# The last four V blocks by token block, the gathered block between the steps, and LayerNorm's scale and shift in two VectorE passes

## The chip, the cores and the metric

One core of a Trainium2 chip runs the whole kernel. The metric is the device time of one execution in microseconds, as the median of several runs. A profile belongs to one execution, whose own time is given beside its span.

## What is computed

The kernel is one layer of an encoder over 512 tokens of width 1024: LayerNorm, a mixer (gated linear recurrence and short convolution), LayerNorm, a PEER expert layer with 16384 one-neuron experts, LayerNorm. The change lies in the end of the expert layer and in the last LayerNorm:

```python
def layer_norm(x, g, b):
    xf = x.astype(jnp.float32)
    mu = jnp.mean(xf, axis=-1, keepdims=True)
    var = jnp.mean(jnp.square(xf - mu), axis=-1, keepdims=True)
    y = (xf - mu) * lax.rsqrt(var + LN_EPS) * g.astype(jnp.float32) + b.astype(jnp.float32)
    return y.astype(x.dtype)

def expert_block(args):
    xb, ib, gb = args
    u = u_tab[ib].astype(x.dtype)
    act = jax.nn.gelu(jnp.einsum("cd,ced->ce", xb, u), approximate=False)
    v = v_tab[ib].astype(x.dtype)
    return jnp.einsum("ce,ced->cd", gb * act, v)

f = peer(h, peer_wq[l], peer_k1[l], peer_k2[l], peer_u[l], peer_v[l])
h = layer_norm(ALPHA * h + f, ln2_g[l], ln2_b[l])
```

## The kernel before

The 512 tokens are four token blocks of 128. For the first three (DT = 3, DTOK = 384 tokens) the expert layer is computed densely: the 16384 experts are 128 blocks of 128 rows, and for each block the activations (gelu of x times the U rows) are multiplied by a matrix of gates and then by the V rows. The fourth block, called gathered here (index DT, `far` in the code), fetches its own rows: GpSimd issues one indirect DMA for each of its 128 slots in either table (L790, L795), and VectorE multiplies and adds them (L808 for U, L812 for V, into the two tiles `gather_sum`).

Stages are blocks of code in which each engine has its own instruction list (L229, L861, L1063, L1334); engines meet at the end of each, where every queue drains. The change lies in the last stage, `experts` (L1241). Its 128 steps take one V block each. Up to TAIL = 64 every second step also makes the activations of a block; from 64 on the steps only load them. The last gathered tile is used in step 111 (TAIL + tail_tiles = 112). Order within a step n is written out by hand for each engine:

- SyncE (L1354): loads of v_raw and g_in for step n + 4 (SLOT = 4 buffers), and of a_in for the step after the next.
- ScalarE (L1432): v_hi of step n + 2 (L1430, float32r half of the V block, waits for y_done of step n - 2, since the four buffers go round), then w_hi of step n (L1449).
- VectorE (L1501): a gathered tile, w = activation times gate (L1520), v_lo of step n + 2 (L1498), w_lo of step n (L1525).
- TensorE (L1407): outputs(n - 1) (L1390): for each of three token blocks and each of the products w_hi v_hi, w_hi v_lo, w_lo v_hi, two matmuls of 512 columns (L1400), 18 in all, accumulated in two PSUM banks per token block. It waits for v_lo and w_lo of its step. In the last step y_ready is raised after each token block.

Then comes the end. VectorE first works on the gathered block (L1535, L1537: 2^0.25 h plus the two sums; L1549, L1551: mean and variance), then on each dense block when y_ready has come (L1545, L1549, L1551). For each block GpSimd computes 1/sqrt(var + eps) and the shift in four operations on one column (L1485 to L1488), ScalarE applies them to 1024 columns (L1458), and the learned scale and shift are two passes (L1327, L1328) that are split by columns: 768 on VectorE (LEFT), 256 on GpSimd (RIGHT). SyncE stores each part (L1383). `Chain` (L76) makes an engine wait for the end of its own instruction. `LAST` is the order of the blocks: gathered, 0, 1, 2.

Of the kernel before, what the change touches and what calls it, by code (L numbers as in the profile page):

```python
# [31 lines left out]
P = 128  # L32
# [1208 lines left out]
def experts(nc, a, sem, bank, h, small, acts, far, act_dram, gates_dram, out):  # L1241
# [9 lines left out]
    STEPS = KEYS  # L1251
    GATHERS = 2 * TURN
# [4 lines left out]
    assert u_turns * GATHERS == SLOTS - U_FROM and 0 <= tail_tiles <= STEPS - TAIL  # L1257
    LAST = (DT, *range(DT))
    LEFT, RIGHT = slice(0, 6 * P), slice(6 * P, D)
# [10 lines left out]
    with ExitStack() as st:  # L1270
# [13 lines left out]
        shift = sb("shift2", [P, TB, 1])  # L1284
# [7 lines left out]
        ln2_loaded, var_ready, rstd_ready, norm_ready, stored = (sem(n) for n in (  # L1292
            "ln2_loaded", "var2_ready", "rstd2_ready", "norm2_ready", "out_stored"))
        y_ready, left_ready, right_ready = sem("y_block_ready"), sem("out_left_ready"), sem("out_right_ready")
        chain, pool_chain = sem("dve_chain_experts"), sem("pool_chain_experts")
# [38 lines left out]
        with nc.Block() as block:  # L1334
            @block.sync
            def _(eng):
# [50 lines left out]
            def _(eng):  # L1387
                mm = nc.tensor.matmul

                def outputs(n, i):  # L1390

                    first, last = (isinstance(n, int) and n == e for e in (0, STEPS - 1))
                    r = i % SLOT
                    eng.wait_ge(v_lo_ready, n + 1)
                    eng.wait_ge(w_lo_ready, n + 1)
                    for tb in range(DT):
                        for w, v, begins, ends in ((w_hi, v_hi, first, False), (w_hi, v_lo, False, False),
                                                   (w_lo, v_hi, False, last)):
                            for half in range(2):
                                ins = mm(bank[2 + 2 * tb + half][:, :], w[r][:, tb * P:(tb + 1) * P],  # L1400
                                         v[r][:, half * HALF_D:(half + 1) * HALF_D], start=begins, stop=ends)
                        if last:
                            ins.then_inc(y_ready, 1)
                    if not last:
                        ins.then_inc(y_done, 1)

                def step(n, i, t, tiles):  # L1407
# [8 lines left out]
                    if not (isinstance(n, int) and n == 0):  # L1416
                        outputs(n - 1, i - 1)

                steps(eng, step)
                outputs(STEPS - 1, STEPS - 1)  # L1420

            @block.scalar
            def _(eng):
# [8 lines left out]
                def step(n, i, t, tiles):  # L1432
# [23 lines left out]
                for at, tb in enumerate(LAST):  # L1456
                    eng.wait_ge(rstd_ready, at + 1)
                    S.activation(h[:, tb, :], h[:, tb, :], ACT.Identity, scale=rs[:, tb, :],  # L1458
                                 bias=shift[:, tb, :]).then_inc(norm_ready, 1)

            @block.gpsimd
            def _(eng):
# [16 lines left out]
                link = Chain(eng, pool_chain)  # L1479
                eng.wait_ge(ln2_loaded, 32)  # L1480
                for at in range(TB + 1):
                    if at < TB:
                        tb = LAST[at]
                        eng.wait_ge(var_ready, at + 1)
                        link(G.tensor_tensor(out=rs[:, tb, :], in0=mv[:, tb, 1:2], in1=small[:, 2:3], op=ALU.add))  # L1485
                        link(G.tensor_tensor(out=rs[:, tb, :], in0=rs[:, tb, :], in1=small[:, 0:1], op=ALU.pow))  # L1486
                        link(G.tensor_tensor(out=shift[:, tb, :], in0=mv[:, tb, 0:1], in1=rs[:, tb, :], op=ALU.mult))
                        G.tensor_tensor(out=shift[:, tb, :], in0=shift[:, tb, :], in1=small[:, 1:2],  # L1488
                                        op=ALU.mult).then_inc(rstd_ready, 1)
                    if at:  # L1490
                        affine(eng, G, link, at - 1, RIGHT, right_ready)

            @block.vector
            def _(eng):
# [6 lines left out]
                def step(n, i, t, tiles):  # L1501
# [20 lines left out]
                    if not (isinstance(n, int) and n + 2 >= STEPS):  # L1522
                        v_lower(n + 2, i + 2)
                    eng.wait_ge(w_hi_ready, n + 1)
                    V.tensor_tensor(out=w_lo[i % SLOT][:, :], in0=w32[:, i % 2, :], in1=w_hi[i % SLOT][:, :].bitcast(F32),  # L1525
                                    op=ALU.subtract).then_inc(w_lo_ready, 1)
                    if more:
                        acts.lower_half(eng, 1, m + 1, r + 1, 0)

# [3 lines left out]
                link = Chain(eng, chain)  # L1533
                eng.wait_ge(ln2_loaded, 32)
                link(V.scalar_tensor_tensor(out=h[:, DT, :], in0=h[:, DT, :], scalar=ALPHA, in1=far.sum[0][:, :],  # L1535
                                            op0=ALU.mult, op1=ALU.add))
                link(V.tensor_tensor(out=h[:, DT, :], in0=h[:, DT, :], in1=far.sum[1][:, :], op=ALU.add))  # L1537
                for at in range(TB + 1):
                    if at < TB:
                        tb = LAST[at]  # L1540
                        if at:
                            eng.wait_ge(y_ready, at)
                            for i in range(2):
                                blk = h[:, tb, i * HALF_D:(i + 1) * HALF_D]
                                ins = V.scalar_tensor_tensor(out=blk, in0=blk, scalar=ALPHA, in1=bank[2 + 2 * tb + i][:, :],  # L1545
                                                             op0=ALU.mult, op1=ALU.add)
                            link(ins)
                        for i in range(2):
                            ins = V.bn_stats(bn[:, tb, i, :], h[:, tb, i * HALF_D:(i + 1) * HALF_D])  # L1549
                        link(ins)  # L1550
                        V.bn_aggr(mv[:, tb, :], bn[:, tb, :, :].rearrange("p a b -> p (a b)")).then_inc(var_ready, 1)  # L1551
                    if at:
                        affine(eng, V, link, at - 1, LEFT, left_ready)
# [23 lines left out]
```

## Time and profile before

| | us |
|---|---|
| median of 3 runs | 1810.9 (1807.27 to 1812.17) |
| profiled execution | 1810.05 |
| its span | 1808.2 |
| TensorE busy in the span | 1690.4 (93%) |
| VectorE busy | 1337.9 (74%) |
| GpSimd busy | 977.7 (54%) |
| ScalarE busy | 740.4 (41%) |

Engines are PE (TensorE matmul), PEld (its weight loads, beside PE), DVE (VectorE), ACT (ScalarE), POOL (GpSimd) and SP (SyncE); a q behind a name is the engine's queue. L12 is line 12 of the kernel. In brackets stands how long the engine sat idle before an instruction, and what released it. Starts and ends are in microseconds from the start of the span; PEclk is the granted TensorE clock as a share of full speed, 2.4 GHz.

### The profile page before, as it was taken

To read this page: it belongs to the slowest core of one execution; us is meant where nothing else is said; L and a number is where in the kernel's file an instruction comes from. 1 tells how busy PE (TensorE), PEld (TensorE's weight loads), DVE (VectorE), ACT (ScalarE), POOL (GpSimd) and SP (SyncE) were. 2 spreads that over 40 slices of the span, in tenths; PEclk is the share of its full clock that TensorE was granted. 3 is DMA by queue.
4 is the path that set the end of the run, shared out by engine and by line. 5 is a ranking of instruction groups with operands and counts; after the bars stand their busy time and mean duration, and the time that the engine had idled before them with its cause. 6 is when DMAs were issued, how large, how long until landed. Compare 5 with 4: busy or idle time off the path is not lost. (4 is left out here: it accounts for less than half of the span.)

```text
span 1808.2 us, 27242 instructions
## 1 busy us (share of the span) xinstructions
PE 1690.4 (93%) x8781; PEld 1461.1 (81%) x8781; DVE 1337.9 (74%) x2430; ACT 740.4 (41%) x1188; POOL 977.7 (54%) x844
## 2 busy tenths in 40 slices
PE   5998889799998999999989997999999999999995
PEld 4776644499998999888988896888888888888884
DVE  7469952368889998599589806778778777888756
ACT  2458750323335455444544443333333333333332
POOL 5635430184436666677667753444666666555303
PEclk8999999899999999999999998999999999999998
DMA  8322100333324557877977798998999989999971
GB/s 263 123 76 70 53 0 0 131 111 111 105 72 136 170 175 252 268 231 226 307 228 232 225 347 316 319 329 311 319 324 322 318 292 328 362 351 356 325 228 62
DMA packets 224428, 396.76 MB, mean 219 GB/s; under 512 B 15256, under 2 KB 155472, under 8 KB 224336
## 3 DMA queue, kind: packets, MB, share of 16 engines
q1 hardware_dynamic: 182512, 258.12, 41.9%
q0 software_dynamic: 36864, 134.23, 22.6%
q10 hardware_dynamic: 4960, 3.24, 0.6%
q8 instruction: 50, 0.82, 0.2%
q14 instruction: 42, 0.34, 0.1%
HBM read 349.40 MB, written 46.14 MB: 219 GB/s over the span
## 5 line engine op out<-in xcount | busy, mean ns | idle before, releaser
L748 POOL TENSOR_TENSOR ut_lo<-gather_sum,ut_hi 128x512 fp32r<-128x512 f32 x194 | 263.3, 1377 | 199.3 <-ACT gather_sum L728 197.9
L708 PE MATMUL bank<-xhi,ut_hi 128*128 128x384 f32 x1024 | 355.8, 347 | 0.0
L708 PE MATMUL bank<-xhi,ut_lo 128*128 128x384 f32 x1024 | 345.1, 337 | 0.0
L708 PE MATMUL bank<-xlo,ut_hi 128*128 128x384 f32 x1024 | 344.7, 337 | 0.0
L1498 DVE TENSOR_TENSOR v_lo<-v_raw,v_hi 128x1024 fp32r<-128x1024 f32 x128 | 156.2, 1220 | 120.8 <-ACT v_hi L1430 120.8
L1400 PE MATMUL bank<-v_hi,w_hi 128*128 128x512 f32 x768 | 241.0, 395 | 4.4 <-DVE w_lo L1525 4.4
L795 POOL DMA_INDIRECT gathered<-in_peer_v,row_index x128 | 182.1, 1423 | 106.5 <-POOLq L794 101.9
L790 POOL COPY row_index<-expert_rows 128x1 int32 (+1 forms) x256 | 174.4, 681 | 120.8 <-DVE gather_product L808 60.0
L1400 PE MATMUL bank<-v_lo,w_hi 128*128 128x512 f32 x768 | 238.0, 391 | 0.0
L1400 PE MATMUL bank<-v_hi,w_lo 128*128 128x512 f32 x768 | 237.2, 390 | 0.0
L1430 ACT ACTIVATE v_hi<-v_raw 128x1024 fp32r<-128x1024 f32 x128 | 135.6, 1059 | 245.9 <-PE bank L1400 234.8
L795 POOL DMA_INDIRECT gathered<-in_peer_u,row_index x128 | 151.3, 1182 | 104.1 <-POOLq L794 103.0
L708 PEld LDWEIGHTS bank<-xlo,ut_hi 128*128 128x128 f32 x1024 | 194.2, 190 | 0.0
L708 PEld LDWEIGHTS bank<-xhi,ut_hi 128*128 128x128 f32 x1024 | 194.2, 190 | 0.0
L708 PEld LDWEIGHTS bank<-xhi,ut_lo 128*128 128x128 f32 x1024 | 193.4, 189 | 0.0
L808 DVE SCALAR_TENSOR_TENSOR gather_product<-gathered,h 128x1024 f32<-128x1024 f32 x128 | 172.9, 1351 | 16.5 <-DMA gathered<-in_peer_u,row_index 9.8
L725 ACT ACTIVATE ut_hi<-bank 128x512 fp32r<-128x512 f32 x256 | 154.9, 605 | 73.1 <-PE bank L696 72.9
L1124 DVE TENSOR_SCALAR first<-iota,selT 128x128 f32<-128x128 f32 x384 | 183.8, 545 | 0.0
L1400 PEld LDWEIGHTS bank<-v_lo,w_hi 128*128 128x128 f32 x768 | 144.8, 188 | 30.8
L1400 PEld LDWEIGHTS bank<-v_hi,w_lo 128*128 128x128 f32 x768 | 144.5, 188 | 30.7
L1400 PEld LDWEIGHTS bank<-v_hi,w_hi 128*128 128x128 f32 x768 | 142.3, 189 | 32.6 <-DVE v_lo L1498 5.0
L696 PE MATMUL bank<-ident,u_raw 128*128 128x128 f32 x1024 | 142.8, 276 | 25.9 <-POOL ut_lo L748 15.7
(182 smaller groups left out, 2855.0 us busy)
## 6 DMA issues: line engine op xcount, KB each, us to landing
u_raw<-in_peer_u SPq DMA_DIRECT2D x128, 512.0 KB, 5.3
v_raw<-in_peer_v SPq DMA_DIRECT2D x128, 512.0 KB, 5.7
g_in<-gate_matrix SPq DMA_DIRECT2D x128, 192.0 KB, 4.2
activations<-gel SPq DMA_DIRECT2D x96, 192.0 KB, 2.0
a_in<-activations SPq DMA_DIRECT2D x96, 192.0 KB, 4.5
gate_matrix<-stage SPq DMA_DIRECT2D x15, 1152.0 KB, 8.0
w_in<-in_w_in SPq DMA_DIRECT2D x28, 512.0 KB, 3.8
wq<-in_peer_wq SPq DMA_DIRECT2D x16, 512.0 KB, 4.2
```

The source lines that it names most:

```text
L696: ins = self.nc.tensor.transpose(self.bank[b][:, k * P:(k + 1) * P], raw[:, j * P:(j + 1) * P], self.ident[:, :])
L708: ins = self.nc.tensor.matmul(self.bank[b + (r % 2) * spare][:, 0:DTOK], u[r % 2][:, k, :], x[:, k, 0:DTOK], start=(i == 0), stop=(i == 3 ...
L725: ins = self.nc.scalar.activation(self.hi[r % 2][at], turned, ACT.Copy)
L748: self.nc.gpsimd.tensor_tensor(out=self.lo[r % 2][at], in0=self.whole[at], in1=self.hi[r % 2][at].bitcast(F32), op=ALU.subtract).then_inc( ...
L790: nc.gpsimd.tensor_copy(self.index[r][:, :], self.rows[:, bass.ds(k, 1)]).then_inc(self.index_ready, 1)
L795: nc.gpsimd.indirect_dma_start(out=self.tile[r][:, :], out_offset=None, in_=self.tables[kind], in_offset=bass.IndirectOffsetOnAxis(ap=self ...
L808: ins = V.scalar_tensor_tensor(out=self.product[:, :], in0=self.tile[r][:, :], scalar=1.0, in1=self.x, op0=ALU.mult, op1=ALU.mult, accum_o ...
L1124: ins = V.tensor_scalar(out=first[:, u, q, :], in0=iota[:, :], scalar1=selT[:, 0, bass.ds(t + q, 1)], scalar2=selT[:, 2, bass.ds(t + q, 1) ...
L1400: ins = mm(bank[2 + 2 * tb + half][:, :], w[r][:, tb * P:(tb + 1) * P], v[r][:, half * HALF_D:(half + 1) * HALF_D], start=begins, stop=ends)
L1430: S.activation(v_hi[r][:, :], v_raw[r][:, :], ACT.Copy).then_inc(v_hi_ready, 1)
L1498: V.tensor_tensor(out=v_lo[r][:, :], in0=v_raw[r][:, :], in1=v_hi[r][:, :].bitcast(F32), op=ALU.subtract).then_inc(v_lo_ready, 1)
```

## The change

- TensorE: the last four steps (CLOSE = 124 on) are no longer done one V block after the other. `closing` takes token block 0 for all four V blocks, then token block 1, then 2, and raises y_ready after each. The waits for v_lo and w_lo of the four steps all stand in token block 0.
- ScalarE and VectorE: v_hi and v_lo of step 127 move from step 125 to step 126, behind w_hi and w_lo of that step.
- The gathered block's residual, statistics, centring and scaling (`far_block`) go into steps 113 to 117 of VectorE, one part at the end of each step.
- The last LayerNorm is (h - mean) * gain and then * rstd + bias, each one scalar_tensor_tensor on VectorE, the second in two halves of 512 columns. VectorE adds epsilon. GpSimd keeps only the power of -0.5, ScalarE has no part.
- SyncE stores halves of 512 columns.

```diff
+    CLOSE = STEPS - SLOT
+    FAR_DONE = TAIL + tail_tiles
-        def affine(eng, engine, link, at, cols, ready):
-            blk = h[:, LAST[at], cols]
-            eng.wait_ge(norm_ready, at + 1)
-            link(engine.tensor_tensor(out=blk, in0=blk, in1=ln[:, 0, cols], op=ALU.mult))
-            engine.tensor_tensor(out=blk, in0=blk, in1=ln[:, 1, cols], op=ALU.add).then_inc(ready, 1)
@@ SyncE @@
                 for at, tb in enumerate(LAST):
-                    for cols, ready in ((RIGHT, right_ready), (LEFT, left_ready)):
-                        eng.wait_ge(ready, at + 1)
+                    for half in range(2):
+                        cols = slice(half * HALF_D, (half + 1) * HALF_D)
+                        eng.wait_ge(out_ready, 2 * at + half + 1)
                         eng.dma_start(out[0, tb * P:(tb + 1) * P, cols], h[:, tb, cols]).then_inc(stored, 16)
@@ TensorE @@
+                def closing():
+                    for tb in range(DT):
+                        for n in range(CLOSE, STEPS):
+                            if tb == 0:
+                                eng.wait_ge(v_lo_ready, n + 1)
+                                eng.wait_ge(w_lo_ready, n + 1)
+                            ins = block_outputs(tb, n % SLOT, False, n == STEPS - 1)
+                        ins.then_inc(y_ready, 1)
-                    if not (isinstance(n, int) and n == 0):
+                    if not (isinstance(n, int) and (n == 0 or n > CLOSE)):
                         outputs(n - 1, i - 1)
                 steps(eng, step)
-                outputs(STEPS - 1, STEPS - 1)
+                closing()
@@ ScalarE @@
-                    if not (isinstance(n, int) and n + 2 >= STEPS):
+                    if not (isinstance(n, int) and n + 2 >= STEPS - 1):
                         v_upper(n + 2, i + 2, loads)
                     S.activation(w_hi[i % SLOT][:, :], w32[:, i % 2, :], ACT.Copy).then_inc(w_hi_ready, 1)
+                    if isinstance(n, int) and n == STEPS - 2:
+                        v_upper(n + 1, i + 1, (n + 1) // SLOT + 1)
-                for at, tb in enumerate(LAST):
-                    eng.wait_ge(rstd_ready, at + 1)
-                    S.activation(h[:, tb, :], h[:, tb, :], ACT.Identity, scale=rs[:, tb, :],
-                                 bias=shift[:, tb, :]).then_inc(norm_ready, 1)
@@ GpSimd @@
-                for at in range(TB + 1):
...
+                for at, tb in enumerate(LAST):
+                    eng.wait_ge(var_ready, at + 1)
+                    G.tensor_tensor(out=rs[:, tb, :], in0=rs[:, tb, :], in1=small[:, 0:1],
+                                    op=ALU.pow).then_inc(rstd_ready, 1)
@@ VectorE, in a step @@
-                    if not (isinstance(n, int) and n + 2 >= STEPS):
+                    if not (isinstance(n, int) and n + 2 >= STEPS - 1):
                         v_lower(n + 2, i + 2)
...
+                    if isinstance(n, int) and n == STEPS - 2:
+                        v_lower(n + 1, i + 1)
+                    if isinstance(n, int) and FAR_DONE <= n < FAR_DONE + 6:
+                        far_block(n - FAR_DONE)
@@ VectorE, the parts @@
+                def moments(tb):
+                    for i in range(2):
+                        ins = V.bn_stats(bn[:, tb, i, :], h[:, tb, i * HALF_D:(i + 1) * HALF_D])
+                    link(ins)
+                    link(V.bn_aggr(mv[:, tb, :], bn[:, tb, :, :].rearrange("p a b -> p (a b)")))
+                    V.tensor_scalar(out=rs[:, tb, :], in0=mv[:, tb, 1:2], scalar1=LN_EPS, scalar2=None,
+                                    op0=ALU.add).then_inc(var_ready, 1)
+                def centre(tb):
+                    link(V.scalar_tensor_tensor(out=h[:, tb, :], in0=h[:, tb, :], scalar=mv[:, tb, 0:1], in1=ln[:, 0, :],
+                                                op0=ALU.subtract, op1=ALU.mult))
+                def spread(tb):
+                    eng.wait_ge(rstd_ready, LAST.index(tb) + 1)
+                    for half in range(2):
+                        cols = slice(half * HALF_D, (half + 1) * HALF_D)
+                        V.scalar_tensor_tensor(out=h[:, tb, cols], in0=h[:, tb, cols], scalar=rs[:, tb, :],
+                                               in1=ln[:, 1, cols], op0=ALU.mult, op1=ALU.add).then_inc(out_ready, 1)
+                def far_block(part):
+                    if part == 1:
+                        link(V.scalar_tensor_tensor(out=h[:, DT, :], in0=h[:, DT, :], scalar=ALPHA, in1=far.sum[0][:, :],
+                                                    op0=ALU.mult, op1=ALU.add))
+                    elif part == 2:
+                        link(V.tensor_tensor(out=h[:, DT, :], in0=h[:, DT, :], in1=far.sum[1][:, :], op=ALU.add))
+                    elif part == 3:
+                        moments(DT)
+                    elif part == 4:
+                        eng.wait_ge(ln2_loaded, 32)
+                        centre(DT)
+                    elif part == 5:
+                        spread(DT)
+                for tb in range(DT):
+                    eng.wait_ge(y_ready, tb + 1)
...
+                    moments(tb)
+                    centre(tb)
+                    spread(tb)
```

## Rows read from the trace of the kernel before

**Rows 1.** The page's head.

```profile
span 1808.2 us, 27242 instructions
```

**Rows 2.** Chain that ended last, in order of time: start us, us, what.

```profile
1525.02 0.14 issue
1525.16 258.67 PE bank L1400 x1140
...
1801.52 1.35 POOLq L1334
```

**Rows 3.** Instructions of L1334: duration ns min/median/max, first and last start us.

```profile
L1334 POOLq DRAIN  x1: 6499/6499/6499, 1801.5 to 1801.5; - x1
...
L1334 SPq DRAIN  x1: 7/7/7, 1805.9 to 1805.9; - x1
```

**Rows 4.** The same of L1063, the stage before.

```profile
L1063 POOLq DRAIN  x1: 8546/8546/8546, 1081.9 to 1081.9; - x1
```

**Rows 5.** Timeline of GpSimd at the end of L1063's stage: start us, us.

```profile
1080.95 2.54 POOL L748 TENSOR_TENSOR ut_lo<-gather_sum,ut_hi 128x512 fp32r<-128x512 f32 x2 [2.53 <-ACT gather_sum L728]
```

**Rows 6.** Timeline of all engines, 1783 to 1799 us: start us, us, what.

```profile
1783.85 1.28 DVE L1545 SCALAR_TENSOR_TENSOR h<-h,bank 128x512 f32<-128x512 f32 x2 [3.56 <-PE bank L1400]
...
1793.00 1.28 DVE L1545 SCALAR_TENSOR_TENSOR h<-h,bank 128x512 f32<-128x512 f32 x2
...
1794.31 1.29 DVE L1549 BATCH_NORM_STATS2 bn<-h 128x6 f32<-128x512 f32 x2
...
1795.63 0.21 DVE L1551 BATCH_NORM_AGGREGATE mv<-bn 128x2 f32<-128x12 f32 x1
...
1796.70 0.96 DVE L1328 TENSOR_TENSOR h<-h,ln 128x768 f32<-128x768 f32 x1
1796.79 1.27 POOL L1486 TENSOR_TENSOR rs<-rs,small 128x1 f32<-128x1 f32 x1
```

**Rows 7.** Timeline of TensorE, 1770 to 1775 us, two of its rows: block starts.

```profile
1770.05 0.62 PE L1400 MATMUL bank<-v_hi,w_hi 128*128 128x512 f32 x2
...
1774.13 0.62 PE L1400 MATMUL bank<-v_hi,w_hi 128*128 128x512 f32 x2
```

**Rows 8.** Timeline of VectorE and ScalarE, 1768 to 1776 us.

```profile
1768.93 0.55 DVE L1520 TENSOR_TENSOR w<-a_in,g_in 128x384 f32<-128x384 f32 x1
...
1770.31 1.06 ACT L1430 ACTIVATE v_hi<-v_raw 128x1024 fp32r<-128x1024 f32 x1 [2.61 <-PE bank L1400]
...
1771.40 1.23 DVE L1498 TENSOR_TENSOR v_lo<-v_raw,v_hi 128x1024 fp32r<-128x1024 f32 x1 [1.92 <-ACT v_hi L1430]
...
1772.54 0.55 DVE L1525 TENSOR_TENSOR w_lo<-w,w_hi 128x384 fp32r<-128x384 f32 x1
...
1773.01 0.55 DVE L1520 TENSOR_TENSOR w<-a_in,g_in 128x384 f32<-128x384 f32 x1
...
1773.59 0.53 ACT L1449 ACTIVATE w_hi<-w 128x384 fp32r<-128x384 f32 x1 [1.81 <-DVE w L1520]
...
1774.15 0.56 DVE L1525 TENSOR_TENSOR w_lo<-w,w_hi 128x384 fp32r<-128x384 f32 x1 [0.59 <-ACT w_hi L1449]
```

**Rows 9.** DMA issues, 1768 to 1776 us: xcount, KB each, median us to landing.

```profile
a_in<-activations SPq DMA_DIRECT2D x1, 192.0 KB, 3.4
```

**Rows 10.** Timeline, 1516 to 1519 us: VectorE's L812 beside GpSimd's L790.

```profile
1516.71 1.28 DVE L812 SCALAR_TENSOR_TENSOR gather_sum<-gathered,expert_gates,gather_sum 128x1024 f32<-128x1024 f32 x1 [0.28 <-DMA gathered<-in_peer_v,row_index]
...
1517.28 0.75 POOL L790 COPY row_index<-expert_rows 128x1 int32<-128x1 int32 x1
```

**Rows 11.** Instructions of L535: duration ns min/median/max.

```profile
L535 DVE TENSOR_SCALAR rms<-bank x2: 151/157/163, 267.2 to 267.2; 128x4 f32<-128x4 f32 x2
```

**Rows 12.** Stretches: length, busy us (x) PE PEld DVE ACT POOL, PEclk, DMA, GB/s.

```profile
952.00:957.10 5.10, 2.99 (x25) 2.80 (x25) 4.96 (x12) 1.14 (x3) 3.57 (x4) 1.00 0.60 202
1039.00:1042.80 3.80, 0.89 (x6) 0.68 (x7) 0.00 (x0) 1.16 (x3) 3.46 (x3) 0.99 1.11 348
1042.80:1046.20 3.40, 3.40 (x14) 3.40 (x13) 0.00 (x0) 1.51 (x3) 2.56 (x2) 0.51 1.05 389
```

More of the change, by code:

```diff
@@ L1291, in experts @@
         y_done = sem("y_step_done")
[L1292 to L1295, printed above, removed]
+        ln2_loaded, var_ready, rstd_ready, stored = (sem(n) for n in (
+            "ln2_loaded", "var2_ready", "rstd2_ready", "out_stored"))
+        y_ready, out_ready = sem("y_block_ready"), sem("out_half_ready")
+        chain = sem("dve_chain_experts")
         def steps(eng, step, between=lambda: None):
@@ L1390, in outputs @@
                 def outputs(n, i):
-                    first, last = (isinstance(n, int) and n == e for e in (0, STEPS - 1))
-                    r = i % SLOT
+                    first = isinstance(n, int) and n == 0
                     eng.wait_ge(v_lo_ready, n + 1)
@@ L1396, in outputs, with block_outputs @@
                     for tb in range(DT):
[L1397 to L1405, printed above, removed]
+                        ins = block_outputs(tb, i % SLOT, first, False)
+                    ins.then_inc(y_done, 1)
+                def block_outputs(tb, r, first, last):
+                    for w, v, begins, ends in ((w_hi, v_hi, first, False), (w_hi, v_lo, False, False),
+                                               (w_lo, v_hi, False, last)):
+                        for half in range(2):
+                            ins = mm(bank[2 + 2 * tb + half][:, :], w[r][:, tb * P:(tb + 1) * P],
+                                     v[r][:, half * HALF_D:(half + 1) * HALF_D], start=begins, stop=ends)
+                    return ins
+                def closing():
[6 more added lines that the diff above has]
+                        ins.then_inc(y_ready, 1)
                 def step(n, i, t, tiles):
@@ L1526, in step @@
                                     op=ALU.subtract).then_inc(w_lo_ready, 1)
+                    if isinstance(n, int) and n == STEPS - 2:
+                        v_lower(n + 1, i + 1)
                     if more:
                         acts.lower_half(eng, 1, m + 1, r + 1, 0)
+                    if isinstance(n, int) and FAR_DONE <= n < FAR_DONE + 6:
+                        far_block(n - FAR_DONE)
+                link = Chain(eng, chain)
+                def moments(tb):
[10 more added lines that the diff above has]
+                    eng.wait_ge(rstd_ready, LAST.index(tb) + 1)
+                    for half in range(2):
+                        cols = slice(half * HALF_D, (half + 1) * HALF_D)
[14 more added lines that the diff above has]
+                        spread(DT)
                 v_lower(0, 0)
@@ L1532, in _ @@
                 steps(eng, step, between=lambda: far.weigh(eng))
[L1533 to L1553, printed above, removed]
+                for tb in range(DT):
+                    eng.wait_ge(y_ready, tb + 1)
+                    for i in range(2):
+                        blk = h[:, tb, i * HALF_D:(i + 1) * HALF_D]
+                        ins = V.scalar_tensor_tensor(out=blk, in0=blk, scalar=ALPHA, in1=bank[2 + 2 * tb + i][:, :],
+                                                     op0=ALU.mult, op1=ALU.add)
+                    link(ins)
+                    moments(tb)
+                    centre(tb)
+                    spread(tb)
 _INS = ["x", "ln_emb_g", "ln_emb_b", "w_in", "lru_conv_w", "lru_conv_b", "lru_wa", "lru_ba", "lru_wx", "lru_bx",
```

16 lines of the change are left out of this document (1 added, 15 removed).

## Prediction

> **What bounds the kernel now.** I read the end of the chain of waits first. Its last long piece is TensorE's matmuls of L1400; after those it runs over VectorE and GpSimd, and its last piece is GpSimd's queue at 1801.52 us [rows 1, 2]. So up to the last matmul TensorE sets the time, and behind it the LayerNorm of the last blocks. Next I read the instructions of L1334, where each engine closes the stage. GpSimd's last arithmetic ends at 1801.52 + 1.35 = 1802.87 us, but its closing DRAIN runs to 1808.05 us (start 1801.5, 6.499 long), 0.15 before the end of the span; SyncE is through at 1805.9 [rows 1 to 3]. The closing of GpSimd, 5.18 us after its last arithmetic, is what ends last. The stage before has the same picture: last GpSimd instruction over at 1083.49 us, DRAIN over at 1081.9 + 8.55 = 1090.45, so 6.96 us later [rows 4, 5]. The time is therefore matmuls, then a serial stretch from the first finished token block (VectorE starts on it at 1783.85) to GpSimd's last instruction, 19.02 us, then 5.33 us of closing [rows 1, 2, 6].
>
> In that stretch VectorE has three token blocks one after the other, and then the last one's way over GpSimd and ScalarE is left.
>
> **Token blocks first.** A V block takes 18 matmuls, 4.08 us from the start of one block to the next, 0.2267 us a matmul [rows 7]. Today token block 0 is complete after 60 of the last 72 matmuls, afterwards after 24. That is 36 x 0.2267 = 8.16 us earlier: 1783.85 - 8.16 = 1775.69 us. Blocks 1 and 2 follow 24 matmuls, 5.44 us, apart: 1781.13 and 1786.57. The number of matmuls and of weight loads stays, so this moves no TensorE time.
>
> **What it demands.** The closing part wants V blocks 124 to 127 within 5.44 us: from its start at 1770.05 us, block 125 at 1771.41, 126 at 1772.77, 127 at 1774.13 [rows 7]. Here the order on ScalarE and VectorE counts. Until w of step 125 (1768.93) nothing changes. Then w_hi(125) no longer stands behind v_hi(127) (1770.31). The steps between starts are, from the rows: w to w_hi 0.58, w_hi to w_lo 0.56, w_lo to the next w 0.47, v_hi to v_lo 1.09, v_lo to the next VectorE instruction 1.14 [rows 8]. So w_hi(125) 1769.51, w_lo(125) 1770.07, w(126) 1770.55, w_hi(126) 1771.13, w_lo(126) 1771.69, over at 1772.25: in time for 125 and 126. On ScalarE v_hi(127) now stands behind w_hi(126) and starts at about 1771.63; behind it are queued v_lo(127) 1772.72, w(127) 1773.86, w_hi(127) 1774.44, w_lo(127) 1775.00. That ends at 1775.55, and with the 0.14 us that the chain shows from the end of a w_lo to the matmul it releases, just ahead of its long piece [rows 2], TensorE can go on at 1775.69 instead of 1774.13. I count a wait of 1.56 us. It shifts the three readiness times to 1777.25, 1782.69 and 1788.13. SyncE's last activation load takes 3.4 us to land [rows 9]; it is released by w(125), over at 1769.48, whose time does not change, so it is there at about 1772.9, ahead of 1773.86.
>
> **The gathered block between steps.** It comes out of the stretch behind the matmuls, where its last two passes lie between the dense blocks, and goes into steps 113 to 117 of VectorE. There VectorE stands idle for 1.92 us in each step before v_lo [rows 8]. The parts are 1.22 to 1.28 us for one pass over 1024 columns [rows 10], and about 1.71 us for the statistics (1.32 + 0.23 + 0.16, below). Each fits into the 1.92; behind them queue w of the next step and, if a part ran over, v_lo and w_lo. w_lo(125) ends 1.04 us before its matmuls at 1774.13, so there are 0.9 us of spare on top [rows 7, 8]. Cost nothing; if the cover were gone, all parts together are 1.24 + 1.24 + 1.71 + 1.30 + 1.34 = 6.8 us. Its two output transfers move ahead of the others on SyncE, at about 1774.4, when the loads are over, and hold nothing up. GpSimd's single pow for it waits with nothing queued behind but the later pows.
>
> **The LayerNorm of blocks 0 to 2.** Per block on VectorE, start to start [rows 6]: residual add 1.31, statistics 1.32, the aggregate with a wait for its end 0.21 + 0.02 = 0.23. Then the new addition of epsilon on a 128x1 tile. The nearest row is a TENSOR_SCALAR of 128x4, 0.157 us [rows 11]; consecutive instructions overlap by 0.09 (v_lo ends 1772.63, w_lo starts 1772.54), so 0.07; bounds 0.05 and 0.23, the aggregate's. Centring, one pass with a scalar from a tile: 1.28 as L812 [rows 10], over two operands in SBUF like that one. Then the wait for GpSimd's pow. The same pow stood beside a multiplication of VectorE from two SBUF tiles: L1328 ends at 1797.66, the pow at 1798.06, so it did its work, 0.40 us, only after VectorE had finished [rows 6]. L790's copy beside L812 shows the same: started 1517.28, over at 1518.03, right behind L812's end 1517.99 [rows 10]. So 0.40, and I take 0.06 to hand over. Last the two halves with the second scalar, 1.34, 1.25 to the next block's start. Sum 1.31 + 1.32 + 0.23 + 0.07 + 1.28 + 0.46 + 1.25 = 5.92 us.
>
> The Trainium skill, SBUF — State Buffer, section "Who interferes with whom", says that a VectorE instruction with two SBUF inputs and a GpSimd instruction that reads SBUF exclude each other for the whole instruction, whoever comes first. The pow rows agree with it. By that rule the 0.46 us is paid in each block, since the centring is issued before the pow can be; without it the pow would be hidden, and that case is the second rival below.
>
> **The sum.** Block 0 starts at 1777.25; block 1 at 1783.17 (its matmuls are over at 1782.69); block 2 at 1789.09 (1788.13). VectorE is what limits here, by 0.5 to 1 us. GpSimd's last pow ends 1.31 + 1.32 + 0.23 + 0.07 + 1.28 + 0.40 = 4.61 us later, at 1793.70, instead of 1802.87: 9.17 us less. Of this 6.60 is the earlier start (8.16 - 1.56), and 2.57 the shorter stretch (16.45 for 19.02). SyncE: last half written at 1795.1; from the last piece ready (1802.87) to its end (1805.9) it took 3.03 us, so 1798.1. GpSimd's DRAIN, 5.18 us after its last work, ends 1798.9 and still sets the end. The profiled execution took 1810.05 us, 1.85 more than its span; less 9.17 this gives 1800.9 us. The median of the three runs is 1810.9, their mean 1810.1, so I do not shift it.
>
> **Rivals.**
> 1. The DRAIN is longer or hangs on the last transfer. With the 6.96 us of the stage before [rows 4, 5] the time is 1802.7; counted from SyncE's end (1808.05 - 1805.9 = 2.15) it is 1798.1 + 2.15 + 0.15 = 1800.4 of span, 1802.3. For it: two DRAINs of different length and no row that says what they wait for.
> 2. The pow slips in under the centring. A block is 5.46 us, the starts 1782.71 and 1788.17, GpSimd over by 1792.4 at the latest: 1799.5. Against it: the pow rows.
> 3. TensorE's wait lets the granted clock fall. From 952.0 to 957.1 us TensorE was busy for 2.99 of 5.10 us and the clock stayed at 1.00, that is 2.4 GHz; from 1039.0 it was busy for 0.89 of 3.80 us, and then the clock was 0.51, 1.2 GHz, for the 3.4 us from 1042.8 [rows 12]. The forecast's wait of 1.56 us between full stretches is nearer to the first. If it fell, 3.4 us at half speed cost 1.7 us, of which 0.5 hide behind VectorE: 1802.1.
> 4. The closing does not follow GpSimd's last work at all, and the end stays at 1810, or the gathered block's cover fails and eats 6.8 us: 1807.7. Against the first: the DRAIN here is open until 2.15 us behind SyncE, with nothing else left to wait for [rows 3].
> 5. Slower. The one mechanism: the last activation tile lands so late that TensorE stands in the closing part and then does the 54 matmuls left at half clock, 54 x 0.2267 = 12.2 us more. Block 2 would be ready at 1800.4, GpSimd over at 1805.0: 1812.2 even with the wait of 1.56. It counts as slower once the wait passes 4.9 us, a landing of about 7.7 us instead of 3.4, in the middle 1816. Against it: the 3.4, and 0.9 us to spare.
>
> **How the numbers follow.** Forecast 0.60; rival 1 0.12; rival 2 0.08; rival 3 0.07; rival 4 0.10; rival 5 0.03. About 0.3% is what a measurement here can tell, 5.4 us, so faster means under 1805.5. The first four cases are faster, 0.87; rival 4 is within, 0.10; slower 0.03. The range takes rivals 1 to 3, with their sizes added on the high side (1800.9 + 1.8 + 1.2 = 1803.9) and 1799.5 on the low; the three runs lie 3.6 below to 1.3 above their median, so I widen by 1 to 2 us: 1797.5 to 1805.0.
>
> **What would show it.** Right: a wait of about 1.5 us on TensorE before block 127's first matmul, released by w_lo; VectorE's first residual add at about 1777.3, blocks 5.9 us apart; GpSimd's pows ending 0.4 us behind the centring; VectorE idle in steps 113 to 117 shrunk from 1.92 us without a gap on TensorE; the DRAIN ending 5.2 us behind the last pow. Wrong: a DRAIN that ends 7 us behind, or at a fixed distance from the transfers; a granted clock of 0.5 before the last matmul; a gap on TensorE before step 124.

## Result: 1799.05 us, and the profile after

| | before | changed |
|---|---|---|
| median of 8 runs, us | 1810.14 (1805.89 to 1814.72) | 1799.05 (1798.07 to 1801.95) |
| profiled execution, us | 1810.05 | 1799.0 |
| its span, us | 1808.2 | 1797.2 |
| first matmul of V block 124, us from the start of the span | 1770.05 | 1767.79 |
| from there to the end of the span, us | 38.2 | 29.4 |

The ratio of the changed kernel to the one before is 0.9945, with a 95% interval of 0.9932 to 0.9958, so 10.0 us less, with 2.4 to either side. The forecast was 1800.9.

The two last lines of the table cut the profile in two. The change touches nothing ahead of step 113, and what lies ahead of V block 124 differs by 2.26 us all the same. The rest, 8.8 us, lies behind it. I call that part the stretch below; it is what the forecast had summed to 9.17.

The timeline of all engines of the changed kernel, from the closing part on. Columns: start us, us, engine, line, operation, tiles, and in brackets the idle time before and what ended it.

```profile
1767.79 0.62 PE L1398 MATMUL bank<-v_hi,w_hi 128*128 128x512 f32 x2
...
1769.30 1.04 ACT L1435 ACTIVATE v_hi<-v_raw 128x1024 fp32r<-128x1024 f32 x1
...
1772.66 0.56 DVE L1519 TENSOR_TENSOR w_lo<-w,w_hi 128x384 fp32r<-128x384 f32 x1 [0.59 <-ACT w_hi L1454]
1773.37 0.70 PE L1398 MATMUL bank<-v_hi,w_hi 128*128 128x512 f32 x2 [1.34 <-DVE w_lo L1519]
...
1775.03 1.29 DVE L1574 SCALAR_TENSOR_TENSOR h<-h,bank 128x512 f32<-128x512 f32 x2 [1.81 <-PE bank L1398]
...
1776.35 1.29 DVE L1533 BATCH_NORM_STATS2 bn<-h 128x6 f32<-128x512 f32 x2
...
1777.67 0.21 DVE L1535 BATCH_NORM_AGGREGATE mv<-bn 128x2 f32<-128x12 f32 x1
1777.92 0.16 DVE L1536 TENSOR_SCALAR rs<-mv 128x1 f32<-128x1 f32 x1
1777.99 1.28 DVE L1541 SCALAR_TENSOR_TENSOR h<-h,mv,ln 128x1024 f32<-128x1024 f32 x1
...
1778.15 1.53 POOL L1484 TENSOR_TENSOR rs<-rs,small 128x1 f32<-128x1 f32 x1 [45.57 <-DVE rs L1536]
...
1779.79 1.42 DVE L1549 SCALAR_TENSOR_TENSOR h<-h,rs,ln 128x512 f32<-128x512 f32 x2 [0.53 <-POOL rs L1484]
...
1781.13 1.28 DVE L1574 SCALAR_TENSOR_TENSOR h<-h,bank 128x512 f32<-128x512 f32 x2
...
1787.20 1.28 DVE L1574 SCALAR_TENSOR_TENSOR h<-h,bank 128x512 f32<-128x512 f32 x2
...
1790.31 1.52 POOL L1484 TENSOR_TENSOR rs<-rs,small 128x1 f32<-128x1 f32 x1 [4.55 <-DVE rs L1536]
1791.94 1.41 DVE L1549 SCALAR_TENSOR_TENSOR h<-h,rs,ln 128x512 f32<-128x512 f32 x2 [0.52 <-POOL rs L1484]
```

Read it downwards. v_hi(127) starts right behind w_hi(126), without the wait that it had before [rows 8]; w_lo(127) ends at 1773.22. TensorE had finished its share of block 126 by then and stood idle for 1.34 us; it goes on 0.15 us later with block 127. VectorE starts on token block 0 at 1775.03, 7.24 us into the stretch; before it was 13.8 [rows 6, 7]. From then on its rows follow each other, but for 0.53 us behind each centring, in which it waits for GpSimd's pow.

The closing instructions of the last stage, same kernel (duration in ns, minimum, median and maximum, then first and last start in us); they answer to [rows 3]:

```profile
L1327 POOLq DRAIN  x1: 6702/6702/6702, 1790.3 to 1790.3; - x1
...
L1327 SPq DRAIN  x1: 7/7/7, 1795.6 to 1795.6; - x1
```

GpSimd's DRAIN ends at 1797.0, 5.14 us behind the end of its last pow (1791.83), and 1.3 us behind SyncE. It still ends last.

The gathered block between the steps, from the timeline of VectorE in steps 115 and 116 (the first three rows are the statistics of the gathered block, the other two belong to the step):

```profile
1729.95 1.28 DVE L1533 BATCH_NORM_STATS2 bn<-h 128x6 f32<-128x512 f32 x2
1731.26 0.21 DVE L1535 BATCH_NORM_AGGREGATE mv<-bn 128x2 f32<-128x12 f32 x1
1731.51 0.15 DVE L1536 TENSOR_SCALAR rs<-mv 128x1 f32<-128x1 f32 x1
1731.59 0.56 DVE L1514 TENSOR_TENSOR w<-a_in,g_in 128x384 f32<-128x384 f32 x1
1732.42 1.23 DVE L1492 TENSOR_TENSOR v_lo<-v_raw,v_hi 128x1024 fp32r<-128x1024 f32 x1 [0.28 <-ACT v_hi L1435]
```

Of the 1.92 us of idle time before v_lo 0.28 are left in the fullest step; v_lo still waits for ScalarE and not for the new work. From 1700 us to the end the only wait that the trace shows for TensorE is the one of 1.3 us before block 127, so the parts cost nothing.

### The profile page after: what moved, and what is told of

Its sections match the earlier page's. It is cut to its first block and busy times, and to the rows that moved or that the text cites. A ratio compares the mean times of both kernels' runs of the same rounds, so it can differ in the third digit from the quotient of the medians.

```text
span 1797.2 us, 27229 instructions
## 1 busy us (share of the span) xinstructions
PE 1691.6 (94%) x8781; PEld 1460.1 (81%) x8781; DVE 1343.7 (75%) x2438; ACT 735.0 (41%) x1184; POOL 971.6 (54%) x824
## 5 line engine op out<-in xcount | busy, mean ns | idle before, releaser
L790 POOL COPY row_index<-expert_rows 128x1 int32 (+1 forms) x256 | 181.4, 708 | 113.0 <-DVE gather_product L808 60.0
```

The lines of the kernel that those rows point to most:

```text
L790: nc.gpsimd.tensor_copy(self.index[r][:, :], self.rows[:, bass.ds(k, 1)]).then_inc(self.index_ready, 1)
```

## Experiments

Each kernel's profile is measured in the same way: the stretch runs from the first matmul of V block 124 to the end of the span. The edits are against the changed kernel unless it says otherwise. The last column is the median of the kernel before, run beside it.

| kernel | stretch, us | expected | median, us | before beside it, us |
|---|---|---|---|---|
| before | 38.2 | | | |
| changed | 29.4 | 29.0 by the forecast | 1799.05 | 1810.14 |
| e1, steps to the end | 36.0 | 36.0 | 1806.61 | 1809.36 |
| e2, block order alone | 34.0 | 33.9 | 1804.62 | 1809.36 |
| e3, v(127) in its old step | 30.3 | 30.2 | 1801.59 | 1809.36 |
| e6, gathered block at the end | 34.8 | 34.7 | 1806.9 | 1809.36 |
| e4, root on ScalarE | 27.2 | 27.1 | 1796.84 | 1808.62 |
| e5, late GpSimd instruction | 31.1 | 31.2 | 1802.38 | 1808.62 |
| e7, pow before centring | 29.0 | 29.9 to 30.3 | 1800.36 | 1808.62 |
| e8, e4 and split waits | 26.6 | 26.5 | 1798.42 | 1808.62 |
| e9, no gathers | 28.1 | 28.0 | 1783.94 (one run) | 1810.06 |
| e10, changed again | 29.4 | 29.4 | 1799.56 | 1810.06 |
| e11, e8 again | 26.6 | 26.6 | 1799.12 | 1810.06 |

### Which part brought it: e1, e2, e6

e1 takes back the order of the matmuls:

```diff
-                    for tb in range(DT):
-                        for n in range(CLOSE, STEPS):
-                            if tb == 0:
-                                eng.wait_ge(v_lo_ready, n + 1)
-                                eng.wait_ge(w_lo_ready, n + 1)
+                    for n in range(CLOSE, STEPS):
+                        eng.wait_ge(v_lo_ready, n + 1)
+                        eng.wait_ge(w_lo_ready, n + 1)
+                        for tb in range(DT):
...
-                        ins.then_inc(y_ready, 1)
+                            if n == STEPS - 1:
+                                ins.then_inc(y_ready, 1)
```

> The changed kernel with one part undone: V blocks 124 to 127 are multiplied one after the other again, y_ready still comes after each token block of the last. I measure from the first matmul of V block 124 to the end of the span: 38.15 us before, 29.41 us in the changed kernel. Theory (the order pays by starting VectorE earlier): TensorE has no wait before block 127, token block 0 is ready 13.8 us in instead of 7.24, VectorE's three blocks still take 6.08 us each, so the stretch is about 36.0 us, 6.5 us longer than the changed kernel and 2.2 shorter than before. Rival (VectorE's passes are the bound whatever the order, and the two-pass LayerNorm brought the gain): the stretch is 29.4 to 30.5 us.

The first matmul of block 124 and VectorE's first instruction on token block 0, from two answers of its timeline:

```profile
1771.65 0.39 PE L1398 MATMUL bank<-v_hi,w_hi 128*128 128x512 f32 x1
```

```profile
1785.45 0.69 DVE L1574 SCALAR_TENSOR_TENSOR h<-h,bank 128x512 f32<-128x512 f32 x1 [8.37 <-PE bank L1398]
```

VectorE starts 13.80 us in and had been idle for 8.37. The stretch is 36.0 us: without the order of the matmuls the two other parts together (gathered block and LayerNorm) are worth 2.2 us, and the order is worth 6.5 on top of them. The rival is out.

e2 is the kernel before with the order of the matmuls and the two moves of step 127 alone (`closing` is that of the change):

```diff
+    CLOSE = STEPS - SLOT
...
-                    if not (isinstance(n, int) and n == 0):
+                    if not (isinstance(n, int) and (n == 0 or n > CLOSE)):
                         outputs(n - 1, i - 1)
...
-                outputs(STEPS - 1, STEPS - 1)
+                closing()
...
+                    if isinstance(n, int) and n == STEPS - 2:
+                        v_upper(n + 1, i + 1, (n + 1) // SLOT + 1)
...
+                    if isinstance(n, int) and n == STEPS - 2:
+                        v_lower(n + 1, i + 1)
```

> The kernel before with one part of the change alone: the last four V blocks by token block, with v_hi and v_lo of step 127 behind w_hi and w_lo of step 126. The gathered block and the LayerNorm stay as before. Theory: VectorE reaches token block 0 only after the gathered block's parts, 9.5 us after the first matmul of block 124 and not at 7.24, so part of the 6.6 us is lost: stretch 33.9 us, 4.2 shorter than before. Rival (the parts add up): 6.6 us shorter than before, 31.5 us.

```profile
1768.82 1.22 DVE L1551 SCALAR_TENSOR_TENSOR h<-h,gather_sum 128x1024 f32<-128x1024 f32 x1
1769.04 0.70 PE L1405 MATMUL bank<-v_hi,w_hi 128*128 128x512 f32 x2 [1.34 <-DVE w_lo L1539]
```

These rows of its timeline show the collision. The matmuls of block 127 and the gathered block's first pass start at the same time; VectorE comes to token block 0 at 1772.78, 9.3 us after the first matmul at 1763.46, and not at 7.24. The stretch is 34.0 us, 4.2 less than before. The order alone thus keeps 4.2 of the 6.6 us it makes room for.

e6 puts the gathered block's parts behind the last step:

```diff
-                    if isinstance(n, int) and FAR_DONE <= n < FAR_DONE + 6:
-                        far_block(n - FAR_DONE)
...
                 steps(eng, step, between=lambda: far.weigh(eng))
+                for part in range(6):
+                    far_block(part)
```

> The changed kernel with the gathered block's five parts behind the last step of VectorE instead of in steps 113 to 117. Theory: they fill the 1.8 us in which VectorE waits for token block 0 and push it by the rest: 7.1 us of parts from the end of w_lo(127), token block 0 starts about 5.3 us later, the stretch is 34.7 us. Rival (the parts lie beside matmuls and cost nothing there either, as TensorE still has 11 us to go): stretch 29.4 to 30.5 us.

From VectorE's timeline:

```profile
1777.20 1.22 DVE L1553 SCALAR_TENSOR_TENSOR h<-h,gather_sum 128x1024 f32<-128x1024 f32 x1
...
1784.49 1.27 DVE L1574 SCALAR_TENSOR_TENSOR h<-h,bank 128x512 f32<-128x512 f32 x2
```

7.3 us of parts stand between the last step and token block 0, which starts 12.64 us into the stretch; the stretch is 34.8. That these parts lie beside busy matmuls is no help: VectorE is the engine that is late there. Moving them is worth 5.4 us once the order and the LayerNorm have changed. e6 also answers a question about the LayerNorm: with the gathered block at the end in both, the new LayerNorm has a stretch of 34.8 us and the old one 34.0 (e2), so there the new one, with the order of the gathered block's passes that goes with it, is 0.8 us slower.

### The wait that the order costs: e3, e8

e3 puts v_hi(127) and v_lo(127) back:

```diff
-                    if not (isinstance(n, int) and n + 2 >= STEPS - 1):
+                    if not (isinstance(n, int) and n + 2 >= STEPS):
...
-                    if isinstance(n, int) and n == STEPS - 2:
-                        v_upper(n + 1, i + 1, (n + 1) // SLOT + 1)
```

and the same for `v_lower`.

> The changed kernel with v_hi and v_lo of step 127 back in step 125. Theory: w_hi(125) and w_lo(125) stand behind v_hi(127) and v_lo(127) again, TensorE waits about 1.8 us before block 125 and a little before 126 and 127, 2.3 us together instead of 1.5; VectorE starts on token block 0 about 0.8 us later and the stretch is 30.2 us instead of 29.4. Rival (block 127's data set the wait in either order): no difference, 29.4 us with one wait of 1.5 us before block 127.

```profile
1772.70 0.70 PE L1398 MATMUL bank<-v_hi,w_hi 128*128 128x512 f32 x2 [1.67 <-DVE w_lo L1517]
...
1774.32 0.71 PE L1398 MATMUL bank<-v_hi,w_hi 128*128 128x512 f32 x2
...
1775.94 0.70 PE L1398 MATMUL bank<-v_hi,w_hi 128*128 128x512 f32 x2
```

In TensorE's timeline the first row is block 125, the others 126 and 127: three blocks come late, 1.62 us apart where 1.36 would do. VectorE starts 8.09 us in, the stretch is 30.3. The two moves are worth 0.8 us.

### GpSimd's pow and its DRAIN: e4, e5, e7, e9

e4 takes GpSimd out of the LayerNorm:

```diff
 @@ ScalarE @@
+                def root(tb):
+                    eng.wait_ge(var_ready, LAST.index(tb) + 1)
+                    S.activation(rs[:, tb, :], rs[:, tb, :], ACT.Sqrt).then_inc(rstd_ready, 1)
...
 @@ GpSimd @@
-                for at, tb in enumerate(LAST):
-                    eng.wait_ge(var_ready, at + 1)
-                    G.tensor_tensor(out=rs[:, tb, :], in0=rs[:, tb, :], in1=small[:, 0:1],
-                                    op=ALU.pow).then_inc(rstd_ready, 1)
 @@ VectorE, spread @@
                     eng.wait_ge(rstd_ready, LAST.index(tb) + 1)
+                    link(V.reciprocal(rs[:, tb, :], rs[:, tb, :]))
```

> The changed kernel without GpSimd in the LayerNorm: ScalarE takes the square root of variance plus epsilon, VectorE its reciprocal on one column, behind the centring. GpSimd's last work is then the last gather, long before. Two things are tested. Theory: the wait of 0.53 us behind each centring goes and a reciprocal of about 0.2 us comes, so the last half is written about 0.9 us earlier; and GpSimd's closing DRAIN, which follows GpSimd's last work by about 5.2 us, is out of the way, so that SyncE's end sets the time: the stretch from the first matmul of block 124 to the end is about 27.1 us instead of 29.41. Rival (the DRAIN ends at a fixed distance behind the output transfers or behind the other engines): it still ends 1.4 us or more behind SyncE, and the stretch is 28.5 us. Second rival (the wait behind the centring is the length of the pow, and the root on ScalarE takes as long): 29.0 us or more.

Its timeline, token block 0 from the centring on, and the closing instructions:

```profile
1777.63 1.28 DVE L1545 SCALAR_TENSOR_TENSOR h<-h,mv,ln 128x1024 f32<-128x1024 f32 x1
1777.75 0.20 ACT L1464 ACTIVATE rs<-rs 128x1 f32<-128x1 f32 x1 [5.47 <-DVE rs L1540]
1778.94 0.16 DVE L1551 RECIPROCAL rs<-rs 128x1 f32<-128x1 f32 x1
1779.14 1.41 DVE L1554 SCALAR_TENSOR_TENSOR h<-h,rs,ln 128x512 f32<-128x512 f32 x2
...
1780.47 1.28 DVE L1579 SCALAR_TENSOR_TENSOR h<-h,bank 128x512 f32<-128x512 f32 x2
```

```profile
L1327 POOLq DRAIN  x1: 9296/9296/9296, 1695.4 to 1695.4; - x1
...
L1327 SPq DRAIN  x1: 7/7/7, 1794.4 to 1794.4; - x1
```

The root runs wholly beside the centring, a block takes 5.80 us where it took 6.10, and the DRAIN was over at 1704.7, long before. SyncE sets the end, 0.2 us before the end of the span (1794.6). Both rivals are out.

e5 adds one instruction and nothing else:

```diff
+                eng.wait_ge(out_ready, 2 * TB)
+                G.memset(pool_tile[:, :], 0.0)
```

> The changed kernel with one memset of one column on GpSimd after the last output half is ready, a tile that nobody reads. Theory (the DRAIN ends about 5.2 us behind GpSimd's last instruction): that instruction ends about 1.7 us later than the last pow did, and the stretch grows from 29.4 to about 31.2 us. Rival (the DRAIN's end hangs on the transfers or on a fixed schedule): no difference, 29.4 us.

```profile
1793.88 0.10 POOL L1488 MEMSET pool_tile<- 128x1 f32 x1 [1.59 <-DVE h L1552]
```

```profile
L1328 POOLq DRAIN  x1: 5246/5246/5246, 1793.9 to 1793.9; - x1
...
L1328 SPq DRAIN  x1: 7/7/7, 1796.1 to 1796.1; - x1
```

A memset of 0.10 us makes the stretch 1.7 us longer. The DRAIN ends at 1799.1, again 5.1 us behind GpSimd's last instruction, while SyncE ends 27.8 us into the stretch as in the changed kernel. So it is GpSimd's last instruction that the end hangs on, and not the output transfers.

e7 makes VectorE wait for the pow ahead of the centring:

```diff
                 def centre(tb):
 
+                    eng.wait_ge(rstd_ready, LAST.index(tb) + 1)
                     link(V.scalar_tensor_tensor(out=h[:, tb, :], in0=h[:, tb, :], scalar=mv[:, tb, 0:1], in1=ln[:, 0, :],
```

> The changed kernel, but VectorE waits for GpSimd's pow before it starts the centring, so that nothing of VectorE runs beside the pow. Theory (the pow's 1.53 us are 0.57 us of work and the time in which VectorE's two SBUF inputs keep it out): each pow takes 0.57 us; VectorE waits about 0.8 us for it before the centring and not after, a block takes about 6.35 us instead of 6.08, the stretch 29.9 to 30.3 us. Rival (this pow takes 1.5 us whoever runs beside it): VectorE waits 1.7 us, a block takes 7.2 us, and the stretch is 32.5 us or more.

```profile
1780.05 0.56 POOL L1484 TENSOR_TENSOR rs<-rs,small 128x1 f32<-128x1 f32 x1 [45.57 <-DVE rs L1536]
1780.64 1.28 DVE L1542 SCALAR_TENSOR_TENSOR h<-h,mv,ln 128x1024 f32<-128x1024 f32 x1 [0.67 <-POOL rs L1484]
1781.96 1.42 DVE L1550 SCALAR_TENSOR_TENSOR h<-h,rs,ln 128x512 f32<-128x512 f32 x2
...
1783.30 1.28 DVE L1575 SCALAR_TENSOR_TENSOR h<-h,bank 128x512 f32<-128x512 f32 x2
```

The pow takes 0.56 us with VectorE standing still and 1.53 us beside the centring. That settles the theory on the pow, and a block takes 6.36 us as expected. The stretch came out otherwise: 29.0 us, shorter than the changed kernel's 29.4 though each block is 0.27 us longer. (The medians of the whole runs, 1800.36 and 1799.05, don't show these 0.4 us.) I had taken it for granted that a slower VectorE makes a later end. The last pow now ends 23.6 us into the stretch instead of 24.0, since it need not sit out the last centring, and the DRAIN follows the pow; SyncE, at 28.7, is still just ahead of it. The miss fits what e4 and e5 say of the DRAIN.

e9 leaves out the indirect transfers, so the experts' share of the fourth token block is missing from its output:

```diff
-        nc.gpsimd.indirect_dma_start(out=self.tile[r][:, :], out_offset=None, in_=self.tables[kind],
-                                     in_offset=bass.IndirectOffsetOnAxis(ap=self.index[r][:, 0:1], axis=0),
-                                     ).then_inc(self.loaded[r], 16)
...
-        eng.wait_ge(self.loaded[r], 16 * loads)
+        eng.wait_ge(self.index_ready, 2 * q + 2)
...
+                        for tile in far.tile:
+                            nc.gpsimd.memset(tile[:, :], 0.0)
```

> The changed kernel without its 256 indirect transfers: GpSimd still writes each row index, VectorE multiplies and adds four tiles that were set to zero once, so the experts' share of the fourth token block is missing from the output. All else stays, the three pows at the end too. In every profile so far the closing DRAIN of GpSimd ended 5.13 to 5.15 us behind its last instruction in the last stage and 6.9 us behind it in the stage before, but at most 0.1 us behind it in the two stages ahead of the first indirect transfer. Theory (the DRAIN is long because GpSimd has issued indirect transfers): here it ends within 0.3 us of the last instruction in all four stages, SyncE's end sets the time, and the stretch from the first matmul of V block 124 to the end is 28.0 us instead of 29.4. Rival (it is long for another reason, the loops or the length of the stage): 5.1 us again and a stretch of 29.4 us.

Its last pow and its closing instructions:

```profile
1776.58 1.52 POOL L1483 TENSOR_TENSOR rs<-rs,small 128x1 f32<-128x1 f32 x1 [4.55 <-DVE rs L1535]
```

```profile
L1326 POOLq DRAIN  x1: 1626/1626/1626, 1776.5 to 1776.5; - x1
...
L1326 SPq DRAIN  x1: 7/7/7, 1781.9 to 1781.9; - x1
```

The DRAIN ends at 1778.2, with the pow and not 5.1 us behind it, and SyncE closes the span (1782.1). In the stage before it ends with the last instruction too, where it took 6.96 us before [rows 4, 5]. So the length of GpSimd's DRAIN belongs to the indirect transfers that it issues. It is no wait for a gather in flight: in the changed kernel the last one is issued at 1695.83 us and lands 7.5 us later, over 80 us ahead of the DRAIN. Nor is 5.14 us a constant. Where the last gather itself is GpSimd's last instruction (e4, e8, e11), the DRAIN ends 7.3, 7.9 and 7.5 us behind it; the expectation of e9, which has 5.13 to 5.15 us for every profile so far, overlooked the first two. What GpSimd does in that time, and why it is 5.14 us in one place, 6.96 in the stage before and over 7 behind a gather, no run shows.

### A version with both, and the changed kernel beside it: e8, e10, e11

e8 is e4 with TensorE's wait split (`part` does the matmuls of the products that it is given):

```diff
                             if tb == 0:
                                 eng.wait_ge(v_lo_ready, n + 1)
+                                eng.wait_ge(w_hi_ready, n + 1)
+                            part(tb, n, ((w_hi, v_hi, False), (w_hi, v_lo, False)))
+                            if tb == 0:
                                 eng.wait_ge(w_lo_ready, n + 1)
-                            ins = block_outputs(tb, n % SLOT, False, n == STEPS - 1)
+                            ins = part(tb, n, ((w_lo, v_hi, True),))
```

> The kernel of e4 with TensorE's wait in the closing part split: the matmuls that need w_hi alone start when w_hi, v_hi and v_lo of their step are there, and only the last two of a step wait for w_lo. Theory: block 127's first matmul starts about 0.6 us earlier, the last two find w_lo ready, VectorE starts on token block 0 about 0.6 us earlier, and since VectorE is what limits from there the whole stretch is 0.6 us shorter than e4's, about 26.5 us; measured against before about 11.6 us less in all. Rival (TensorE or the transfers limit the end once GpSimd is out): no difference to e4.

```profile
1773.47 0.56 DVE L1534 TENSOR_TENSOR w_lo<-w,w_hi 128x384 fp32r<-128x384 f32 x1 [0.59 <-ACT w_hi L1465]
1773.58 0.69 PE L1407 MATMUL bank<-v_hi,w_hi 128*128 128x512 f32 x2 [0.75 <-ACT w_hi L1465]
```

Block 127's first matmuls now run beside w_lo(127). VectorE starts 6.64 us in, and the stretch is 26.6 us, 0.6 less than e4's. Its median, 1798.42 us, is above e4's 1796.84 all the same.

e10 is the changed kernel and e11 is e8, with no edit.

> The changed kernel once more, beside the next one and on the same chip, to compare the two: about 10 us less than before, stretch 29.4 us. How far its first matmul of V block 124 lies from the 1767.8 us of its first profile shows what the part that the change leaves alone scatters by.

> The kernel of e8 once more, square root on ScalarE and split waits, beside the changed kernel. Theory: 2.8 us less than the changed kernel, as its stretch of 26.6 us for 29.4 says. Rival: what the stretch gains is lost in the scatter ahead of it, and the medians lie within 1 us of each other or the wrong way round.

e10 was 1799.56, e11 1799.12 us, on one chip. Over both sessions e8 and e11 have a mean of 1798.85 in 12 runs, the changed kernel 1799.94 in 14, with standard deviations of 2.3 and 2.5 us. By the stretch e8 is 2.8 us ahead in both of its profiles; by the times of whole runs it is 1.1 us ahead with a standard error of 0.9, which excludes neither nothing nor 2.8. The rival of e11, medians within 1 us of each other, is what came. e11's profile shows how: its first matmul of V block 124 came at 1774.39 us, 8.6 us later than e10's at 1765.83.

That place lies between 1763.5 and 1774.4 us in the twelve profiles with gathers, before and changed among them. Most of the scatter arises in one stage. GpSimd's DRAIN starts at 550.5 to 553.3 us in the stage of L861, but at 1076.3 to 1086.4 in that of L1063; from there to V block 124 it is 687.0 to 688.2 us in each. The code there is the same in all twelve. The traces explain a part of it: in that stage TensorE's granted clock was at 1.2 GHz for 3.4 us in e10 and for 10.2 us in e11, and for 3.4 to 13.7 us over the twelve. Had TensorE been the limit all that time, half of it would be lost, 1.7 to 6.8 us (an estimate). With that taken off, ten of the twelve stages agree within 3.2 us; e2's remains 0.9 us shorter than those and e11's 2.8 us longer. e9 is through the stage in 517.6 us, the others in 525.8 to 534.4, so the gathers lengthen it. No run here asks what varies in it from one execution to the next.

## Why the prediction was right, step by step

**The bound.** TensorE up to the last matmuls, then VectorE's chain, then GpSimd's DRAIN: all three held. The reading that the DRAIN ends last came from two rows [rows 3, 4], and rival 1 stood against it with 0.12. e5 and e4 settle that its end follows GpSimd's last instruction, e9 that its length comes with the gathers. In all nine profiles whose last stage has gathers and GpSimd's last instruction in the LayerNorm or behind it, it closed 5.13 to 5.15 us behind that instruction. That holds for the kernel before too, where the forecast read 5.18.

**The order of the matmuls.** 8.16 us earlier less a wait of 1.56 was forecast. The gap between block 126 and 127 on TensorE is 1.50 us, and VectorE's start at 7.24 us into the stretch stands against a forecast of 7.20. The steps between starts on ScalarE and VectorE [rows 8], put in their new order by hand, gave this wait to within 0.06 us.

**The gathered block.** Forecast at no cost; 0.28 us of idle time are left in the fullest step, where 1.92 - 1.71 = 0.21 was worked out.

**LayerNorm.** Here lies the miss of the sum: 8.78 us (8.8 above) for 9.17. A block was forecast at 5.92 us and took 6.10 and 6.07. The wait for the aggregate's end cost 0.25 for 0.23, the hand-over from GpSimd 0.11 for 0.06, and the two halves with a scalar from a tile 1.34 us to the next start for 1.25; that last term I had made from L1545, whose scalar is an immediate. Residual add, statistics and centring were right to 0.01, and so was the pow's 0.41 behind the centring. The two blocks make 0.33 of the 0.39; VectorE's start, 0.04 later than forecast, and the way from its third start to the last pow's end, 4.63 us for 4.61, make the rest.

**The clock.** The granted clock stayed at full speed through the wait, so rival 3 did not come. The stretches of the changed kernel (length, busy us with counts of PE, PEld, DVE, ACT, POOL, then the granted clock, DMA share, GB/s):

```profile
1767.80:1773.20 5.40, 4.23 (x19) 3.18 (x17) 3.82 (x6) 2.00 (x3) 0.00 (x0) 1.00 0.18 55
1773.20:1786.50 13.30, 12.53 (x54) 10.06 (x54) 10.24 (x18) 0.00 (x0) 3.05 (x2) 1.00 0.20 74
```

**The rest of the difference.** The median fell by 11.1 us, the stretch by 8.8. Over all runs of this study the kernel before has a mean of 1809.55 us (65 runs), the changed one 1799.94 (14 runs): 9.6 us, with a standard error of 0.75 from the two standard deviations of 2.6 and 2.5. What is above 8.8 is within that, and no saving was found ahead of V block 124. That the median came out at the time of rival 2 is chance: the pow did not slip in under the centring.

**The parts.** The three are no sum. From 38.2 us the order of the matmuls alone brings 4.2, the other two alone 2.2, all together 8.8. The order makes VectorE late from token block 0 on, and only then is it worth much to clear VectorE of the gathered block. What the new LayerNorm brings by itself in the changed kernel no run shows; the one comparison that there is, e6 with e2, has it 0.8 us slower.

The Trainium skill, SBUF — State Buffer, section "Who interferes with whom", has the rule that the prediction cited for the pow, an exclusive lock for the length of the instruction, granted to the first. e7 bears it out with 0.56 us alone and 1.53 beside the centring.

## What to carry to other kernels

Look at what each engine's queue still does after its last arithmetic: here a one-column instruction on GpSimd was followed by 5.1 us of closing, and of the 2.2 us that it brought to take that instruction elsewhere (e4), 1.3 were the closing and 0.9 the shorter chain on VectorE. When a reduction ends in a serial epilogue, finish its output blocks one after the other in the last steps, and move whatever already stands in the epilogue's engine ahead of it in the same change: the order alone gave 4.2 us, the rest without it 2.2, all together 8.8. And measure from a mark behind the part that scatters: the stretch agreed within 0.02 us in both kernels profiled twice, while whole runs of 1800 us scattered by 2.5.

## What was not expected of the hardware

- GpSimd's closing DRAIN takes 5.1 us behind its last instruction in the last stage, 7.3 to 7.9 where that instruction is a gather (e4, e8, e11), and 6.96 in the stage before, and 0.1 us or less with the indirect transfers left out (e9). The forecast used the figure without its cause.
- A scalar_tensor_tensor of two times 512 columns takes 1.42 us with its scalar from a tile and the second operand from SBUF, and 1.28 us with an immediate and the second operand from PSUM, both in the changed kernel. One of 1024 columns takes 1.28 us with a scalar from a tile, and 1.22 with an immediate (e6).
- To let VectorE wait can bring the end forward, here by 0.4 us in the stretch (e7, one profile), where the end hangs on another engine that VectorE locks out.
